# A hybrid decoder step on one core: all expert scores first, then all expert outputs, with the routing beside the scores

## What is computed

```python
def peer_route(h, w_q, sub_keys):          # 8 heads, product keys 2 x 128
    q = (h @ w_q).reshape(T, PEER_HEADS, 2, PEER_DK)
    s = jnp.einsum('thpd,hpkd->thpk', q, sub_keys)
    sv, si = lax.top_k(s, PEER_TOPK)       # 16 of 128, for both halves
    cand = sv[:, :, 0, :, None] + sv[:, :, 1, None, :]
    cv, ci = lax.top_k(cand.reshape(...), PEER_TOPK)   # 16 of 256
    ...                                    # ia, ib: the two key numbers of each choice
    return ia * N_KEYS + ib, jax.nn.softmax(cv, axis=-1)

    act = jax.nn.gelu(jnp.einsum('td,thkd->thk', hi, eu[ii]))
    y = jnp.einsum('thk,thkd->td', act * gi, ev[ii])
```

## Time and profile before

| | |
|---|---|
| time, median of 3 runs | 3394.63 us (3391.62 to 3402.66) |
| span of the profiled execution | 3393.9 us |
| query projection ends | 1453.8 us into the span |
| routing | to about 1584 us |
| gate weights, first half | to about 1674 us |
| 128 units, first half | to about 2419 us |
| gate weights, second half | to about 2510 us |
| 128 units, second half | to about 3255 us |
| norm, `ple`, output | to 3393.9 us |

### The profile page before, as it was taken

The page is one execution under the profiler, slowest core; times in us unless marked ns, Lnnn a source line. Parts: engine busy times, 40 slices in busy tenths (PEclk is TensorE's granted clock), DMA queues, the critical chain, the costliest instruction groups (busy, mean ns, idle before and its releaser), DMA issues.

```text
span 3393.9 us, 63208 instructions
## 1 busy us (share of the span) xinstructions
PE 3112.1 (92%) x23603; PEld 2921.9 (86%) x23603; DVE 1973.4 (58%) x3888; ACT 1291.3 (38%) x2225; POOL 190.1 (6%) x203
## 2 busy tenths in 40 slices
PE   6999899799999998922899999999889999999989
PEld 6999689499755787922799999999889999999979
DVE  4477466422233235488766666666766666666654
ACT  4455320122222024411544444444444444444444
POOL 0000110000000000002400000000330000000000
PEclk8999899599999999966999999999999999999989
DMA  5555200356576444400155455455225554545543
GB/s 192 177 184 180 85 1 8 127 199 245 200 250 214 185 160 148 173 0 0 70 180 184 177 182 182 177 185 175 73 99 176 184 179 180 184 175 185 178 148 125
DMA packets 82022, 519.76 MB, mean 153 GB/s; under 512 B 9186, under 2 KB 9458, under 8 KB 28914
## 3 DMA queue, kind: packets, MB, share of 16 engines
q1 hardware_dynamic: 69394, 468.36, 38.8%
q0 software_dynamic: 11360, 45.61, 3.7%
q10 hardware_dynamic: 1152, 4.19, 0.3%
HBM read 508.74 MB, written 9.39 MB: 153 GB/s over the span
## 4 chain that ended last, share of the span: by engine, by line
PE 88%; DVE 7%; POOL 2%; SPq 2%; issue 1%; ACT 0%; DMA 0%; POOLq 0%; DVEq 0%; ACTq 0%
PE ps L551 23%; PE ps L552 23%; PE ps L553 22%; PE ps L915 3%; PE ps L858 3%; PE ps L869 3%; PE ps L978 2%; POOL arena L1335 2%; PE ps L732 1%; SPq L465 1%; PE ps L611 1%; DVE arena L1865 1%; PE ps L546 1%; PE ps L720 1%; PE ps L603 1%
## 5 line engine op out<-in xcount | busy, mean ns | idle before, releaser
L551 PE MATMUL ps<-split 128*128 128x264 f32 x6288 | 1798.0, 286 | 53.9 <-DVE split L393 53.9
L552 PE MATMUL ps<-split 128*128 128x264 f32 x6288 | 1789.7, 285 | 0.0
L553 PE MATMUL ps<-split 128*128 128x264 f32 x6288 | 1784.7, 284 | 0.0
L393 DVE TENSOR_TENSOR split<-arena,split 128x512 fp32r<-128x512 f32 x1568 | 1078.6, 691 | 956.9 <-ACT split L388 954.1
L388 ACT ACTIVATE split<-arena 128x512 fp32r<-128x512 f32 x1568 | 987.8, 632 | 1401.5 <-PE ps L553 1401.1
L551 PEld LDWEIGHTS ps<-split 128*128 128x128 f32 x6288 | 1187.9, 189 | 73.9 <-issue 36.2
L552 PEld LDWEIGHTS ps<-split 128*128 128x128 f32 x6288 | 1188.3, 189 | 0.8
L553 PEld LDWEIGHTS ps<-split 128*128 128x128 f32 x6288 | 1183.6, 188 | 0.3
L1910 DVE TENSOR_TENSOR arena<-arena,ps 128x264 f32<-128x264 f32 x512 | 216.4, 423 | 5.9 <-PE ps L553 5.9
L1335 POOL TENSOR_TENSOR arena<-arena 128x512 f32<-128x512 f32 x66 | 121.7, 1844 | 1264.6 <-DVE arena L1865 1264.6
L978 PE MATMUL ps<-arena 128*128 128x128 f32 x1056 | 140.3, 287 | 38.9 <-POOL arena L1335 38.8
(11 more groups left out here) (299 smaller groups left out, 1696.4 us busy)
## 6 DMA issues: line engine op xcount, KB each, us to landing
arena<-in_wd SPq DMA_DIRECT2D x280, 1024.0 KB, 4.8
arena<-in_vd SPq DMA_DIRECT2D x128, 1024.0 KB, 4.8
arena<-in_kx POOLq DMA_DIRECT2D x32, 512.0 KB, 6.4
arena<-in_kx SPq DMA_DIRECT2D x32, 512.0 KB, 4.5
arena<-in_vx SPq DMA_DIRECT2D x32, 512.0 KB, 4.3
arena<-in_vx POOLq DMA_DIRECT2D x32, 512.0 KB, 4.4
arena<-in_state POOLq DMA_DIRECT2D x8, 512.0 KB, 6.7
o_ss<-arena ACTq DMA_DIRECT2D x8, 512.0 KB, 7.5
```

The lines of the kernel that those rows point to most:

```text
L393: nc.vector.tensor_tensor(ckl(q), at(WR + (s % 4) * D_MODEL + q * QW, QW), as_f32(ckh(q)), ALU.subtract).then_inc(lo_ready, 1)
L551: mm(out, wh, xh, start=start, stop=False)
L552: mm(out, wh, xl, start=False, stop=False)
L553: return mm(out, wl, xh, start=False, stop=stop)
```

## The change

The two halves become one pass. All 128 score units run first (`u`), unrolled, then all 128 output units (`v`) in 16 groups of 8. Between them the scores live in DRAM (`gd`), and so do the gate weights (`wdr`).

- Routing runs beside the score units. PE makes the key scores of tile 0 ahead of unit 0; those of tiles 1 and 2 and the three transposes stand behind units 2, 19, 19, 36 and 41, in PSUM banks 4 to 7, which the score units do not use. On DVE the routing instructions are interleaved with the units' low parts: `beside(us)` counts declared work and issues one low part for every 0.8 us of it, and `lows_until` forces them up to a unit ahead of a wait.
- Gate weights are built for all 128 first keys in 66 steps of 4 tokens behind units 44 to 65 and 76 to 97 (2, 1, 2, 1 steps a unit). For a step POOL makes 8 one-hot rows times gate (`tensor_scalar`, 128 elements: high and low part of the gate for each token), DVE one one-hot matrix of 512 elements, PE four fp32r matmuls of 256 columns, ACT copies the high half with a stride of 132 floats into `WST` (`take_high`), DVE adds the low half (`take_weights`). Each pass of 33 steps is then written to DRAM by four DMAs on SP, behind the load of unit 72 and of unit 104; in DRAM a run is 132 floats, 528 bytes.
- Scores: ACT writes Gelu into a ring of four buffers; every second unit SP writes two of them to DRAM (270 KB).
- Output phase: POOL loads scores and gate weights of a group (2 x 1.08 MB), multiplies them (8 instructions of 264 elements), ACT takes the high part (`split_weighed`), DVE the rest (`rest_weighed`), for group g + 1 during group g, one of 8 blocks in each unit. PE waits for all 8 at the start of a group (`a_blk`). A block of outputs now sums 8 experts' blocks over two quarters, so DVE adds to `xt3` twice a unit, not four times; `peer_v` is laid out in DRAM to match.

The diff, cut to its core:

```diff
 LEVELS = 7
 RING = 4
 QK = KT // RING
-HALF = N_KEYS // 2
 PGW = NH * P
-EG = 4
...
-STREAM = [("A", 56), ("gates", 32), ("up", 16), ("out", 16), ("wq", 16), ("peer0", 128), ("peer1", 128), ("ple", 16)]
+EG = 8
+GROUPS = N_KEYS // EG
+WT = 4
+W_STEPS = T // WT
+W_PASS = (33, 33)
+PT_W = W_PASS[0] * WT
+KEYS1, SCORES1, SCORES2 = 2, 8, 26
+EXP_AT = (13, 30, 38)
+TURN_AT = (19, 36, 41)
...
+W_FROM = (44, 76)
+SPILL_AT = (72, 104)
+def w_unit(g):
+    p, i = (0, g) if g < W_PASS[0] else (1, g - W_PASS[0])
+    return W_FROM[p] + 4 * (i // 6) + (0, 0, 1, 2, 2, 3)[i % 6]
+def w_steps_after(k):
+    return [g for g in range(W_STEPS) if w_unit(g) == k]
+STREAM = [("A", 56), ("gates", 32), ("up", 16), ("out", 16), ("wq", 16), ("u", 128), ("v", 128), ("ple", 16)]
 S0 = {}
 _n = 0
 for _name, _c in STREAM:
...
+        mg_step = sem("merge_step")
+        gd = nc.dram_tensor("scores_spill", (P, N_KEYS * T), F32, kind="Internal").ap()
+        wdr = nc.dram_tensor("gates_spill", (P, N_KEYS * T), F32, kind="Internal").ap()
         def wait_done(eng, n):
...
+            return at(WST, N_KEYS * PT_W).rearrange("p (a t) -> p t a", t=PT_W)[:, t0:t0 + WT, :]
+        ghi = lambda g, j: at(GB + ((g % 2) * EG + j) * T, T)
+        whi = lambda g, j: at(WB + ((g % 2) * EG + j) * T, T)
+        a_high = lambda g, j: sp_(ABUF[g % 2] + j * T, T)
+        a_low = lambda g, j: sp_(ABUF[g % 2] + (EG + j) * T, T)
         class Chain:
...
-                            load_w(it, 4, s, (wd, vd)[kind], ((u0 + 4) + j, v0 + j)[kind])
-                with sp.Fori(0, 15) as it:
-                    group(it)
+            def write_scores(k):
+                wait_evac(sp, JOB["u"] + k + 1)
+                sp.dma_start(gd[:, k * T:(k + 2) * T], at(GST + (k % 4) * T, 2 * T)).then_inc(g_saved[(k // 2) % 2], 16)
+            for k in range(N_KEYS):
+                wait_slot(sp, 0, 0, S0["u"] + k - RING)
+                load_w(0, 0, S0["u"] + k, wd, 136 + k)
+                if k >= 6 and k % 2 == 0:
+                    write_scores(k - 6)
+                for p_ in range(2):
+                    if k == SPILL_AT[p_]:
+                        n = W_PASS[p_] * WT
+                        sp.wait_ge(w_out, W_PASS[0] + p_ * W_PASS[1])
+                        for h in range(4):
+                            a = 32 * h
+                            sp.dma_start(wdr.rearrange("p (a t) -> p a t", t=T)[:, a:a + 32, p_ * PT_W:p_ * PT_W + n],
+                                         at(WST + a * PT_W, 32 * PT_W).rearrange("p (a t) -> p a t", t=PT_W)[:, :, 0:n]
+                                         ).then_inc(w_saved[p_], 16)
+            for k in range(RING):
+                wait_slot(sp, 0, 0, S0["v"] + k - RING)
+                load_w(0, 0, S0["v"] + k, vd, k)
+                write_scores(N_KEYS - 6 + 2 * k) if k < 3 else None
+            with sp.Fori(1, 32) as it:
...
+            def build_weights(g):
+                if g < 2:
+                    for b in range(4):
+                        pe.wait_ge(route_free[b], 3)
+                else:
+                    pe.wait_ge(w_out, g - 1)
+                pe.wait_ge(ohb_ready, g + 1)
+                pe.wait_ge(oha_ready, g + 1)
+                for t in range(WT):
+                    last = mm(w_banks(g)[:, t // 2, (t % 2) * 256:(t % 2 + 1) * 256], sp_(OHB + ((g % 3) * WT + t) * P, P),
+                              sp_(GA + ((g % 2) * WT + t) * 256, 256), start=True, stop=True)
+                last.then_inc(w_built, 1)
             key_scores(0)
-            key_scores(1)
...
+            for k in range(N_KEYS):
+                split_unit(0, 4, S0["u"] + k, JOB["u"] + k)
+                if k == KEYS1:
+                    key_scores(1)
+                for c in range(3):
+                    if k == TURN_AT[c]:
+                        turn_results(c)
+                if k == TURN_AT[0]:
+                    key_scores(2)
+                for g in w_steps_after(k):
+                    build_weights(g)
+            def outputs(it, m, s, g):
+                pe.wait_ge(a_blk, it * m + EG * (g + 1))
+                for dq in range(EG):
+                    for q in range(RING):
+                        d = 2 * dq + q // 2
+                        if q % 2 == 0:
+                            pe.wait_ge(y_added, it * (2 * m) + (16 * g + d + 1))
+                        wait_low_part(pe, it, m, s + dq, q)
+                        for i in range(RING):
+                            j = RING * (q % 2) + i
+                            last = products(ps[:, 4 + d % 4, 0:T], ckh(q)[:, i * P:(i + 1) * P], ckl(q)[:, i * P:(i + 1) * P],
+                                            a_high(g, j), a_low(g, j), j == 0, j == EG - 1)
+                        last.then_inc(quarter_done, 1)
+            pe.wait_ge(w_out, W_STEPS)
+            with pe.Fori(0, GROUPS // 2) as it:
+                for b in range(2):
+                    outputs(it, 2 * EG, S0["v"] + EG * b, b)
...
-                        act.wait_ge(pe_job, it * 8 + PJ[n])
-                        A(wh3[:, bass.ds(it * 32 + 4 * (n - wb), 4), :],
-                          bank(n).rearrange("p (t r a) -> p t r a", t=4, r=2)[:, :, 0, :], ACT.Copy).then_inc(evac[n % 4], 1)
-                with act.Fori(0, 8) as it:
-                    for j in range(4):
-                        weights_of(it, j)
-                weights_of(8, 0)
...
-                        for q in range(RING):
+            def take_high(g):
+                act.wait_ge(w_built, g + 1)
+                if g == W_PASS[0]:
+                    act.wait_ge(w_saved[0], 64)
+                A(w_stage(g), w_bank(g, 0), ACT.Copy).then_inc(w_high, 1)
+            def split_weighed(it, m, g, j):
+                act.wait_ge(am_ready, it * m + (EG * g + j + 1))
+                A(a_high(g, j), ghi(g, j), ACT.Copy).then_inc(ah_ready, 1)
+            for q in range(RING):
+                high_part(act, 0, 0, S0["u"], q)
+            take_scores(0)
+            for k in range(N_KEYS):
+                for q in range(RING):
+                    high_part(act, 0, 0, S0["u"] + k + 1, q)
+                wait_quarter(act, 0, 0, S0["u"] + k, RING - 1)
+                if k >= 4 and k % 2 == 0:
+                    act.wait_ge(g_saved[(k // 2) % 2], 16 * (k // 4))
+                n = JOB["u"] + k
+                A(at(GST + (k % 4) * T, T), bank(n)[:, 0:T], ACT.Gelu).then_inc(evac[n % 4], 1)
+                if k == SCORES1:
+                    take_scores(1)
+                if k == SCORES2:
+                    take_scores(2)
+                for c in range(3):
+                    if k == EXP_AT[c]:
+                        gate_exp(c)
+                for g in w_steps_after(k):
+                    take_high(g)
+                if k >= N_KEYS - EG:
+                    split_weighed(0, 0, 0, k - (N_KEYS - EG))
...
+            def values(it, m, s, g, last=False):
+                for j in range(EG):
+                    for q in range(RING):
+                        if not (last and j == EG - 1):
                             high_part(act, it, m, s + j + 1, q)
-                        wait_quarter(act, it, m, s + j, RING - 1)
...
-                values(0, 0, s0 + 124, True)
+                    if not last:
+                        split_weighed(it, m, g + 1, j)
...
-                    for j in range(4):
-                        gate_rows(it, j)
-                gate_rows(8, 0)
-            pool.wait_ge(y_added, 516)
+            pool.wait_ge(gate_rest, 1)
+            for g in range(W_STEPS):
+                if g >= 2:
+                    pool.wait_ge(w_built, g - 1)
+                for t in range(WT):
+                    n = g * WT + t
+                    for i, gate in enumerate((as_f32(sp_(GHI + n, 1)), at(GLO + n, 1))):
+                        ins = nc.gpsimd.tensor_scalar(sp_(GA + ((g % 2) * WT + t) * 256 + i * P, P), cst(C_IOTA),
+                                                      at(IDX + n, 1), gate, ALU.is_equal, ALU.mult)
+                ins.then_inc(oha_ready, 1)
+            def load_group(g):
+                pool.dma_start(at(GB + (g % 2) * EG * T, EG * T), gd[:, g * EG * T:(g + 1) * EG * T]).then_inc(gw_in[g % 2], 16)
+                pool.dma_start(at(WB + (g % 2) * EG * T, EG * T), wdr[:, g * EG * T:(g + 1) * EG * T]).then_inc(gw_in[g % 2], 16)
+            for p_ in range(2):
+                pool.wait_ge(w_saved[p_], 64)
+            for g in range(GROUPS):
+                if g == 0:
+                    for n in range(2):
+                        for b in range(2):
+                            pool.wait_ge(g_saved[b], 16 * (2 * n + 2))
+                        load_group(n)
+                pool.wait_ge(gw_in[g % 2], 32 * (g // 2 + 1))
+                for j in range(EG):
+                    nc.gpsimd.tensor_tensor(ghi(g, j), ghi(g, j), whi(g, j), ALU.mult).then_inc(am_ready, 1)
+                if g + 2 < GROUPS:
+                    for b in range(2):
```

(63 more changed lines are left out.)

293 lines of the change are left out of this document (96 added, 197 removed).

## The result

| | median | runs | ratio to before, 95% interval |
|---|---|---|---|
| before | 3397.4 us | 4, 3391.62 to 3402.66 | |
| changed kernel | 3441.8 us | 4, 3438.54 to 3450.92 | 1.0128 [1.0110, 1.0146] |
| forecast | 3219 us | range 3150 to 3310 | |

The forecast had the wrong sign: 176 us less was expected, 44 us more came.

A forecast was written before the change was run, and what follows sets the result against it. PE was taken to bound the units, not the stretches between. Removing 312.2 us and adding 136.4 (15.4 + 35 + 3 + 46 + 37) gave 3393.9 - 175.8 + 0.7 = 3219 us, range 3150 to 3310.

The forecast's parts named there:

- what hides the rest of a step: Gate-weight steps: ACT, DVE and POOL work fits under PE's 6.55 us a unit, POOL taking 4.2; cost nothing.
- the shared port: Rival, units with steps: POOL excludes DVE's two-input instructions, 8.0 us a unit, 64 us more, 3283 us; chance 0.12.
- the removed 312 us: Stretches not bound by PE, before the first half and between the halves: 220.4 and 91.8 us, 312.2 taken away.
- the units at 5.82: The 256 score and output units stay, bound by PE, at 5.82 us each as in both halves before.
- routing beside the score units: Score units with DVE's routing interleaved: 3 us, 0 to 15; rival that it is not hidden, 3250 us, chance 0.07.
- the write of the gate weights: DRAM write after each pass: 38 us, delaying the next load; stall 20.9 and clock 2 us, twice, sum 46.
- writes and loads mix: Rival, gate-weight writes on SP's queue: they mix with the loads, nothing stalls, 46 us less, 3173 us; chance 0.12.
- The rival of the short runs: Gate-weight writes: 144 ns a packet whatever its length, 147 us a write, PE stalls 130 us twice, 3437 us; chance 0.07.
- the start of a group: Output phase: PE waits 2.3 us for the eighth weighed block at each of 16 group starts, 37 us; lower end 29.
- score writes and group loads cost nothing: DRAM traffic of 17 MB and 35 MB: at nothing, 205 to 220 GB/s in all against 420, loads three units ahead.

The follow-up runs named there:

- e3: Changed kernel with POOL's comparison replaced by a multiplication, same two pointers, so the gate weights are wrong; 3324.5 us.
- e7: Changed kernel with the four one-hot rows of the gate's high part made by DVE, not POOL, same output; 3324.7 us, 0.9774 of the kernel before.
- e11: Changed kernel with the turn of PE's output loop moved into the middle of a group; 3427.0 us, 1.0083 of the kernel before.
- e8: Changed kernel with high-part rows on DVE, gate weights written in long runs and the next group's blocks a unit earlier; 3286.9 us, 0.9653 of the kernel before.

## Why the prediction was wrong, step by step

- **Failed: what hides the rest of a step.** "POOL: eight tensor_scalars took 2.80, 1.5 x 2.80 = 4.2. All fit, and POOL works two steps ahead; cost nothing". The row shows instructions with the same name, shape and engine, but with another operation and one pointer fewer. In this form the eight take 7.55 us, 11.3 a unit, and the two passes became POOL's: 11.1 us a unit (233.4 / 21) where 6.55 were forecast, +186 us in all, the whole change of sign. The step put a price at nothing because 4.2 is less than 6.55, and gave no upper end to a form of instruction that no row showed; an upper end of twice the price would have reached 8.4 and made POOL a rival with a chance of its own.
- **Right in mechanism, and the smaller part of the cause: the shared port.** POOL's instruction is on average 0.16 us longer than alone in the changed kernel, 0.24 in e3, 0.41 in e7 (mean 1.192 against 0.783). Without it eight would take 6.28 us, 9.4 a unit, still over 6.55; by that estimate the price alone makes 42 x 2.87 = 120 of the 186 us and the blocking most of the rest. The rival put the port at 64 us; it is 56 once POOL's instruction is cheap. The row that it was read from is weaker than the prediction took it: that DVE instruction (L1865) needs 0.685 us at its shortest in the trace of before, not 0.55, so it lost some 0.2 us and not all of the 0.33 of the overlap. The Trainium skill (*SBUF — State Buffer*, Who interferes with whom) names this exclusion. POOL's 1.73 us beside 0.79 in one run of instructions agrees.
- **Right: the removed 312 us** and the units at 5.82: beside the routing PE is now busy 281 of 287 us, and with POOL relieved the stretch takes 367.8 us where 366.0 were worked out.
- **Right: routing beside the score units**, 3.7 us over the forecast for the whole stage, of which the routing was given 3.
- **Nearly right: the write of the gate weights.** A stall of 20.9 us and 2 of clock each was forecast; PE stood 17.0 and 17.4 us, and behind the first its matmuls came every 0.22 us, not 0.12, for 2.6 us more. The write took 34.9 us where 38 were worked out, and 38 ns a packet where 37 were. That writes and loads mix was refuted: from 2000 to 2030 the queue moved the write alone, and the load's packets began only as it ended. The rival of the short runs gave 3437 us, near what came, but by 147 us a write and stalls of 130 us that do not exist; the figure agrees by accident.
- **Half right: the start of a group.** The 2.3 us were worked out to the tenth for nine of the starts. The seven at the loop's turns take 4.5: 51.6 us in place of 37. The clock behind them was not in the sum at all: 0.97 over 750 us is some 22 us. The two make about the +37.4 of that stage.
- **Right: score writes and group loads cost nothing** that PE waits for.

## What to carry to other kernels

Take the price of an instruction from a row with the same operation and operands, not only the same name and shape; where there is none, give its upper end a rival if the engine's sum comes near the bound with it. When work is moved beside a loop, sum every engine for one turn and ask which one is next, with the time that engines cost each other added. And where a wait stays after its cause is gone, look at what else falls on that place, here the turn of a loop and the fetch of its code.

## What the runs showed of the hardware

- POOL's tensor_scalar over 128 elements takes 0.78 us with a comparison, 0.44 with multiplications, at two pointers each; the same compare form takes 0.345 on DVE. The compare form took 1.01 us on average beside DVE's low parts (both inputs in SBUF), and beside DVE's add from PSUM 0.787, as alone.
- Writes to DRAM in runs of 528 bytes moved 278 GB/s with full DMA engines, in runs of 16.9 KB 431 GB/s; and SP stood 26 us at issuing four of the first kind, 4.7 us at four of the second.
- A turn of PE's loop of 16 units left PE idle 4.5 us where 16 KB packets of code were fetched again at the turn, also where everything it waits for was there, and 0 in e11, where none were; in e7 and e8 another 0.5 to 4.1 us stood ten matmuls behind it, again with such a packet. Moving the loads away changed nothing. Why one loop is fetched again and the other is not is open.
